# Early routing of prompt rows, dense sample columns and 88-row tiles in a two-layer expert kernel

## The reference, cut to what matters

```python
s = sigmoid(t @ w_router)                        # 16 experts in 4 groups
# group with the largest sum of its two best (s + bias); the two best experts in it
w = s[idx] / s[idx].sum()
h = silu(t @ w_gate[e]) * (t @ w_up[e])          # 1024 -> 512
y = sum over the two experts of w * (h @ w_down[e])   # 512 -> 1024
```

## Time and profile before

| | us |
|---|---|
| three runs | 1125.22 median, 1124.78 to 1127.2 |
| the profiled execution, its own time | 1126.03 |
| its span, first to last instruction | 1124.4 |
| PE busy | 978.1 (87%) |
| DVE busy | 376.1 (33%) |
| ACT busy | 195.2 (17%) |
| POOL busy | 94.5 (8%) |
| bytes moved | 296.26 MB, 263 GB/s in the mean |

### The profile page before, as it was taken

The page is one execution under the profiler, slowest core; times in us unless marked ns, Lnnn a source line. Parts: engine busy times, 40 slices in busy tenths (PEclk is TensorE's granted clock), DMA queues, the critical chain, the costliest instruction groups (busy, mean ns, idle before and its releaser), DMA issues.

```text
span 1124.4 us, 36091 instructions
## 1 busy us (share of the span) xinstructions
PE 978.1 (87%) x15881; PEld 836.7 (74%) x15881; DVE 376.1 (33%) x825; ACT 195.2 (17%) x441; POOL 94.5 (8%) x179
## 2 busy tenths in 40 slices
PE   7979999989998329999999997783399999999975
PEld 6857777754566128999999996562389999999962
DVE  1234443423364612122122122796112122122127
ACT  1233434430052020000000001111200000001010
POOL 0002112141010030000000001200200000000011
PEclk8989999999999559999999999895699999999998
DMA  9513244614311979999999995790599999999935
GB/s 336 189 54 91 89 135 127 206 43 137 92 48 64 412 272 332 361 405 380 403 388 397 381 389 189 269 354 9 194 368 366 407 388 391 393 380 384 396 118 201
DMA packets 80249, 296.26 MB, mean 263 GB/s; under 512 B 10200, under 2 KB 40288, under 8 KB 71871
## 3 DMA queue, kind: packets, MB, share of 16 engines
q1 hardware_dynamic: 52343, 246.53, 58.5%
q10 hardware_dynamic: 19712, 26.75, 7.1%
q0 software_dynamic: 8144, 22.29, 5.7%
HBM read 255.88 MB, written 40.11 MB: 263 GB/s over the span
## 4 chain that ended last, share of the span: by engine, by line
PE 79%; DVE 10%; DMA 4%; issue 3%; POOL 2%; ACT 1%; ACTq 0%; SPq 0%; POOLq 0%; DVEq 0%
PE PS L924 16%; PE PS L945 15%; PE PS L934 15%; PE PS L840 5%; PE PS L598 4%; PE PS L910 3%; PE PS L645 3%; PE PS L661 2%; PE PS L554 2%; PE PS L654 2%; PE PS L576 2%; POOL expert_rows L1106 2%; PE PS L749 1%; PE PS L618 1%; PE PS L635 1%
## 5 line engine op out<-in xcount | busy, mean ns | idle before, releaser
L924 PE MATMUL PS<-arena,ring 128*64 128x96 f32 x4096 | 185.4, 249 | 52.6 <-DVE arena L1759 52.4
L924 PEld LDWEIGHTS PS<-arena,ring 128*64 128x64 f32 x4096 | 175.1, 139 | 59.3 <-issue 59.3
L945 PE MATMUL PS<-arena,ring 128*64 128x96 f32 x4096 | 175.4, 246 | 2.5 <-issue 2.0
L934 PE MATMUL PS<-arena,ring 128*64 128x96 f32 x4096 | 175.0, 246 | 2.8 <-issue 2.8
L945 PEld LDWEIGHTS PS<-arena,ring 128*64 128x64 f32 x4096 | 171.3, 137 | 3.2 <-issue 2.5
L934 PEld LDWEIGHTS PS<-arena,ring 128*64 128x64 f32 x4096 | 171.2, 137 | 3.1 <-issue 3.1
L1759 DVE STREAM_TRANSPOSE arena<-arena 128x768 uint32<-128x768 uint32 x34 | 54.2, 1595 | 166.7 <-ACT arena L1311 138.4
L1784 DVE COPY arena<-PS 128x384 f32<-128x384 f32 x32 | 17.9, 558 | 164.3 <-PE PS L945 164.3
L1313 ACT ACTIVATE arena<-PS 128x384 f32<-128x384 f32 x32 | 15.7, 490 | 265.5 <-PE PS L945 265.5
L840 PE MATMUL PS<-ring,arena 128*128 128x512 f32 x128 | 55.6, 593 | 0.7 <-issue 0.7
L598 PE MATMUL PS<-arena,ring 128*128 128x260 f32 x192 | 46.8, 395 | 2.3 <-POOL ring L1057 2.0
(11 more groups left out here) (276 smaller groups left out, 1030.1 us busy)
## 6 DMA issues: line engine op xcount, KB each, us to landing
ring<-w_gate SPq DMA_DIRECT2D x32, 2048.0 KB, 14.8
ring<-w_up SPq DMA_DIRECT2D x32, 2048.0 KB, 16.1
ring<-w_down SPq DMA_DIRECT2D x32, 2048.0 KB, 17.9
arena<-expert_rows ACTq DMA_DIRECT2D x144, 96.0 KB, 9.0
expert_out<-arena ACTq DMA_DIRECT2D x32, 384.0 KB, 11.8
expert_rows<-ring SPq DMA_DIRECT2D x6, 1920.0 KB, 10.2
ring<-cache_ckv SPq DMA_DIRECT2D x56, 128.0 KB, 2.2
ring<-w_o SPq DMA_DIRECT2D x1, 4096.0 KB, 19.3
```

What stands on the lines that cost most here:

```text
L924: last = nc.tensor.matmul(bank(s, KF, CAP)[at:at + 64, f, :], wg[w][:, k, P * f + at:P * f + at + 64], xeT[s][:, k, :], start=(k == 0), st ...
L934: last = nc.tensor.matmul(out[at:at + 64, :], wu[w][:, k, P * f + at:P * f + at + 64], xeT[s][:, k, :], start=(k == 0), stop=(k == KD - 1))
L945: last = nc.tensor.matmul(bank(4 + m // 4, 4, CAP)[at:at + 64, m % 4, :], wd[w][:, f, P * m + at:P * m + at + 64], h[s][:, f, :], start=(f ...
```

## The change

Three things are changed together.

1. **Early routing.** `route` is split into `choose` (two best experts) and `assign` (slots, indices, tables), each over a range of row blocks. In layer one they run for the four prompt blocks inside `samples()`: `router(0, 3)` moves to batch 1, `choose` behind `sample_pair(1)`, the counting matmuls to PE's batch 2, `assign` behind `sample_pair(2)`. POOL scatters the prompt rows right then (8 of 10 transfers), SP instead of ACT loads the first two tiles, and SP issues the first weights in another order, each as soon as its part of the ring is free. ACT scales the prompt rows before the samples' norm.
2. **Dense sample columns.** The sample rows are routed after the loop has begun. Experts 0 and 1 (tiles 0 and 1, outside of the loop now) compute all 8 sample rows as 8 more columns (WIDE = 104), with an output block of their own (`yT_s`, `ys_s`, 16 rows in `yd`). For the other experts 8 slots are kept free (`reserve`). `choose` and `assign` for the sample block run on DVE during tile 0; their scatter is waited for by ACT in tile 1, before it loads tile 2.
3. **Rows per tile.** ROWS = (96, 88): layer two's tiles stand 88 slots apart, an expert overflows beyond 88 rows, and the gate, up and down matmuls, the silu, the products and the copies there take 88 columns. The load of a tile's input stays at 96 rows; the store is 88 rows. Two more overflow tiles are provided for (NOV = 12).

The diff, cut to its core:

```diff
-NOV = 10
+NOV = 12
+DENSE = 2
+WIDE = CAP + DB
+ROWS = (CAP, 88)
@@ SP, first weights of layer one
-                    load_expert(0, 0, 1, gate_free=(pv_ps, BATCHES + 1))
-                    load_expert(0, 1, 0, gate_free=(mix_ps, NT), down_free=(lg_ps, 1))
+                    sp.wait_ge(pv_ps, 3)
+                    sp.dma_start(wu[1], t["w_up"][0, 0].rearrange("(p k) f -> p k f", p=P)).then_inc(q["wu_ld"][1], 16)
+                    sp.wait_ge(pv_ps, 4)
+                    sp.dma_start(wd[1], t["w_down"][0, 0].rearrange("(k p) d -> p k d", p=P)).then_inc(q["wd_ld"][1], 16)
+                    sp.wait_ge(sc_ps, BATCHES)
+                    sp.dma_start(wd[0], t["w_down"][0, 1].rearrange("(k p) d -> p k d", p=P)).then_inc(q["wd_ld"][0], 16)
+                    sp.wait_ge(pv_ps, 5)
+                    sp.dma_start(wg[1], t["w_gate"][0, 0].rearrange("(p k) f -> p k f", p=P)).then_inc(q["wg_ld"][1], 16)
+                    sp.wait_ge(scat, 128)
+                    load_rows(sp, 0, 0, slice(0, CAP))
+                    load_rows(sp, 0, 1, slice(CAP, 2 * CAP))
+                    sp.wait_ge(mix_ps, NT)
+                    sp.dma_start(wg[0], t["w_gate"][0, 1].rearrange("(p k) f -> p k f", p=P)).then_inc(q["wg_ld"][0], 16)
+                    sp.dma_start(wu[0], t["w_up"][0, 1].rearrange("(p k) f -> p k f", p=P)).then_inc(q["wu_ld"][0], 16)
@@ PE, samples()
-                    if u == BATCHES - 1:
+                    if u == 1:
+                        pe.wait_ge(tp_ev[0], 15)
+                        pe.wait_ge(tp_ev[1], 15)
                         router(0, 3)
+                    elif u == 2:
+                        counts(1, 0, NT - 1)
@@ PE, experts(L)
+                if L == 0:
+                    pe.sem_inc(q["back_ps"], 1)
+                    pe.wait_ge(dense, 2)
+                    tile(0, 0, WIDE)
+                    tile(0, 1, WIDE)
+                    turn_sample_out()
-                with pe.Fori(0, nh) as u:
+                with pe.Fori(1 if L == 0 else 0, nh) as u:
@@ PE, before experts(0)
             mix(0, 4)
+            turn_sample_rows()
             router(0, 4)
-            counts(0)
             experts(0)
@@ DVE, samples()
+                    elif u == 1:
+                        v.memset(r_exp[:, E * (NT - 1):], 1.0).then_inc(lg_zero, 1)
+                        choose(0, 1, 0, NT - 1)
+                    elif u == 2:
+                        assign(0, 1, 0, NT - 1)
@@ PE, tile: every matmul of the three products
-                                last = nc.tensor.matmul(bank(s, KF, CAP)[at:at + 64, f, :], wg[w][:, k, P * f + at:P * f + at + 64],
-                                                        xeT[s][:, k, :], start=(k == 0), stop=(k == KD - 1))
+                                last = nc.tensor.matmul(bank(s, KF, n)[at:at + 64, f, 0:m], wg[w][:, k, P * f + at:P * f + at + 64],
+                                                        x[:, k, :], start=(k == 0), stop=(k == KD - 1))
@@ ACT, behind the four batches
+                act.wait_ge(scat, 128)
+                for i in range(NT - 1):
+                    scale_rows(i)
@@ ACT, tile
+                    if n == WIDE and s:
+                        act.wait_ge(scat, 160)
+                        load_rows(act, L, 0, slice(2 * CAP, 3 * CAP))
+                        scale_rows(NT - 1)
```

More of the change, by code:

```diff
@@ L954, in tile @@
                     down(4, (KF - 1,))
-                    for m in (1, 2, 3, 5, 6, 7):
-                        last = down(m, range(KF))
-                        if m in (3, 7):
+                    for c in (1, 2, 3, 5, 6, 7):
+                        last = down(c, range(KF))
+                        if c in (3, 7):
                             last.then_inc(q["down_ps"][s], 1)
@@ L1035, in _ @@
                 router(1, i)
-            counts(1)
+            counts(3, 0, NT)
             experts(1)
@@ L1348, in samples @@
                         take_latent_out(u - 1)
-                    if u == BATCHES - 2:
+                    if u == 1:
                         take_rows(0, 3)
+                        act.wait_ge(lg_ps, 1)
+                        nc.scalar.activation(r_exp[:, 0:E * (NT - 1)], bank(6, E * (NT - 1)), ACT.Exp, scale=-1.0
+                                             ).then_inc(lg_exp, 1)
                 take_latent_out(BATCHES - 1)
+                act.wait_ge(scat, 128)
+                for i in range(NT - 1):
+                    scale_rows(i)
             deviation(0, 0, 0)
@@ new lines, in by_group, with choose, tiles @@
+            def by_group(a):
+                return a.rearrange("p (a b) -> p a b", b=EPG)
+            def choose(L, n, a, b):
+                T, cols, groups = b - a, slice(E * a, E * b), slice(GROUPS * a, GROUPS * b)
+                over = [P, T, E]
+                def tiles(r):
+                    return r[:, cols].rearrange("p (a b) -> p a b", a=T)
+                dve.wait_ge(lg_exp, n)
+                link(v.tensor_scalar_add(r_exp[:, cols], r_exp[:, cols], 1.0))
+                link(v.reciprocal(r_s[:, cols], r_exp[:, cols]))
+                if n == 1:
+                    dve.wait_ge(router_ld, 32)
+                link(v.tensor_tensor(tiles(r_bias), tiles(r_s), bias_row.unsqueeze(1).to_broadcast(over), ALU.add))
+                b4 = by_group(r_bias[:, cols])
+                sums = r_m6.rearrange("p (a b) -> p a b", b=6)[:, groups, :]
+                cmp = r_big.rearrange("p (a j i) -> p a j i", j=EPG, i=2 * EPG)[:, groups, :, :]
+                wide = [P, T * GROUPS, EPG, EPG]
@@ new lines, in tile @@
+                    if n == WIDE and s == 0:
+                        assign(0, 2, NT - 1, NT)
+                    elif n == WIDE:
+                        next_rows()
+                    dve.wait_ge(q["down_ps"][s], 2 * u + 2)
+                    if n == WIDE:
+                        v.tensor_copy(yT_s[:, 4:8, DB * s:DB * (s + 1)], bank(5, 4, n)[:, :, CAP:])
+                    v.tensor_copy(yT[:, 4:8, 0:ROWS[L]], bank(5, 4, n)[:, :, 0:ROWS[L]]).then_inc(q["yT_set"], 1)
+                tile(0, 0, False, CAP if L else WIDE)
@@ L1820, in _ @@
                     norm(1, 0, step - 4)
-            route(1)
+            choose(1, 3, 0, NT)
+            assign(1, 3, 0, NT)
             dve.wait_ge(mix_ps, 2 * NT)
```

400 lines of the change are left out of this document (225 added, 175 removed).

## The result

The changed kernel takes 1143.2 us in the median (1139.33 to 1144.68), the kernel before beside it on the same chip 1125.07. The ratio is 1.0153, 95% interval 1.0131 to 1.0175: **slower by 1.5%**, where I had forecast 1109.5, 1.4% faster. The profiled execution has a span of 1143.0 us and an own time of 1144.68, the longest of the four.

What follows compares the result with a forecast made beforehand. Layer one's loop waits on the samples' routing chain; layer two is bound by transfers. Early start -18.8, loop one +5.4, between layers +0.3, layer two -2.8 sum to -15.9 us: 1109.5 us forecast, range 1101 to 1119.

Steps and rivals of the forecast that it cites:

- Layer two, -2.8: Layer two's loop: 88 rows a tile save 2.8 us, bounds 0 and 7, because transfers bind rather than PE.
- the store is 32 KB of 7.1 MB smaller (13 x 0.1 us = 1.3): Layer two's output store: fewer bytes per tile save 1.3 us over thirteen tiles, part of the 2.8 us.
- paid in full: Rival, 6%: in layer two transfers have room, so PE's saving of 17.7 us counts whole; 1092 us.
- pace does not follow the columns: Rival, 3%: weight loads set PE's pace, so layer two keeps 17.0 us a tile, -0.3 instead of -2.8; 1112 us.
- overflow: Rival, 4%: an expert in layer two exceeds 88 rows, adding two tiles, 36.8 us; 1146 us.
- turned at about 431, wanted at 434: Layer one, tile 2: its input rows are ready in time; if that cover is gone, a wait up to 4 us.
- The third rival: 15%: early routing gives little, through costlier batches, late tile 2 rows or cold code; together 8 to 12 us less, 1117 to 1121.
- They land by 377. Not on the path.: The eight early prompt scatters before layer one's loop: landed by 377, the two tiles' rows by 385, delaying nothing.
- Low clock, 1.5: Samples' stage after the batches: PE's idle gap brings the lower clock sooner, costing 1.5 us, bounds 0 and 4.
- The batches, 11.9: Samples' batches: routing work in DVE's queue ends the samples' stage 11.9 us later, bounds 10 to 14.
- Cold code, 3.0: Layer one's loop, entered after two unrolled tiles: code is new twice, costing 3.0 us, bounds 0 and 8.
- don't bind here: Layer one's loop: transfers don't set its pace, since they start 20 us earlier as well.

Runs made afterwards that it cites:

- e4: Changed kernel with layer two's 88-row store cut into one transfer of 80 rows and one of 8; 1132.9 us, ratio 1.0063 to the kernel before.
- e11: Kernel before, without early routing, with 88 columns in layer two's matmuls and copies but slots and stores of 96 rows; 1124.7 us, ratio 0.9984.
- e15: e13 with only w_gate of tile 0 and w_down of tile 1 issued behind the prompt scatters' landing; 1116.7 us, ratio 0.9903 to the kernel before.
- e8: e3 with assign's weights and tables moved behind the samples' values and ACT's scalings behind the norm; 1130.3 us, ratio 1.0026 to the kernel before.
- e7: e3 with POOL's two broadcast loads at tile 5 and tile 3's rows issued only when tile 2's are turned; 1124.9 us, ratio 0.9993.
- e5: Changed kernel with latent_q in 64 half-width records in place of 32 full-width ones; 1138.4 us, ratio 1.0093 to the kernel before.
- e9: e3 plus the changes of e5, e7 and e8, and tile 1's output copied before tile 2's rows are turned; 1121.2 us, ratio 0.9959.
- e12: e3 with tile 1's output copied before tile 2's rows are turned and POOL's two broadcast loads at tile 5; 1126.8 us, ratio 0.9978.
- e3: Changed kernel with 88 columns in layer two but slots, capacity and stores at 96 rows; 1134.2 us, ratio 1.0056 to the kernel before.
- e14: e13 with w_gate and w_down of tile 0 and w_down of tile 1 issued only behind the prompt scatters' landing; 1116.9 us, ratio 0.9910.
- e13: e9 with ACT issuing tile 3's rows behind tile 1's output copies, not ahead of them; 1116.7 us, ratio 0.9899 to the kernel before.

## Why the prediction was wrong, step by step

The median is 33.7 us above the forecast. The two largest steps that failed stand first.

- **Layer two, -2.8: measured +8.4.** The failed step is "the store is 32 KB of 7.1 MB smaller (13 x 0.1 us = 1.3)". I priced the store by its bytes; as one transfer of 88 rows it is cut into 11 shares and not 16 (the packet counts above), and every tile took 0.56 us longer than with 80 + 8 rows (e4). The rest was right: with 96-row stores the columns alone give -3.3 in the kernel before (e11), 18.28 us a tile against my 18.4, 37.9 ns a record. One premise of the sum was not: that transfers are served more slowly with a deep queue (see the last section). The rivals "paid in full", "pace does not follow the columns" and "overflow" are all refuted; none of them was this mechanism, and my bounds, 0 to -7, ended on its other side.
- **The rows of tile 2, "turned at about 431, wanted at 434".** Turned at 455.5, and 12.1 us of that are the later start of the loop; wanted at 446.6. In the trace before, sixteen such loads around the loop's start (405 to 445) land in 2.4 us in the median, and I counted with little more. Here they go out beside 2 MB weights with four more row loads and two broadcasts about them, and the broadcasts I had not counted at all. My "up to 4 us" was 9.5 of idle time. The third rival named this cause, too small. The same wait carried loop one past my own sign of being wrong (over 288).
- **"They land by 377. Not on the path."** The scatters landed at 396.4 (e15 shows why), and held first ACT, 1.7 us, and with that gone the rows (e8).
- **latent_q** stood in the change and had no term: 2 to 3.5 us. `mix(0, 3)` behind it ran 2.3 us longer at the lower clock, which had no term either, and whose cause is open.
- **Low clock, 1.5:** 3.3 in the samples' values and projection (0.51 over 370 to 394). Inside its bounds.
- **The batches, 11.9:** 12.0 measured, partly by luck: batch by batch +3.2, +2.4 and +6.4 against my +3.0, +3.5 and +5.3, so two errors of 1 us cancel. My sign "above 401 (the batches cost more)" came true for other reasons. Right were between the loops (0.3 against 0.1), 44.6 ns at 104 columns, 1.7 for the sample output (1.8 in e7), no overflow tile, and tile 0 not waiting for the sample's routing.
- **Cold code, 3.0:** four stalls put down to issue in the first four tiles, 4.65 us in all, against three of 2.53 before: 2.1 more. In bounds; that they are code arriving is my reading, which no run tests.
- **The loop's transfers, "don't bind here":** true of the profiled execution up to its last tile (0.55 us), but not of e5, whose last four tiles took 18.7 to 19.0 us, nor of e9 and e12 to e15.

In sum the early routing with the dense columns does move the first gate record forward, by 11.7 us in the median of seven traces against three without it (402.1 against 413.8; 6.7 in the profiled execution, 18.8 forecast), and loop one loses some 15 to 17 again; e7 gives 9.1 of that back against e3.

## What to carry to other kernels

When a tile's row count changes, read how each of its transfers is cut, not only its bytes: a row count with a poor divisor on one small store can cost more than the columns save. Price small transfers by the queue that they will stand in at their new time; a latency read in a quiet stretch says nothing beside weight loads. And once weights run at their limit, a faster start can be worth nothing in the end, as in e14 and e15, so ask first how much lead the ring has.

## What was not expected of the hardware

- 352 KB a tile stored as one transfer of 88 rows made the loop 8.7 us longer than the same rows stored as 80 and 8, with the DMA share at 1.02 in both; the packets of 4 bytes are 11 a store in the one and 24 in the other.
- Scatters of 128 rows land in 6.7 us with one 2 MB transfer ahead of them (e15) and in 8.8 to 18.0 with three about them (e13); 96 KB row loads in 6.4 us beside weights, in 19.7 with two 512 KB broadcasts and four more loads about them.
- 32 records of 16 columns with 128 columns of weights take 4.1 us at a granted clock of 0.90 (e3, 127 ns each) and up to 5.7 at a lower one; 64 records with 64 columns take 2.0 us (e5, 32 ns each, clock 0.99).
- In e3 the transfers were slow in passing: w_down landed every 19.8 us for two tiles from 914 to 954, and every 17.9 us from 971 to 1079 with 30 us from issue to landing. e11 has the same, 19.6 us twice from 911 to 950; the cause is open. A deep queue was not served more slowly, against what I had read from the earlier trace rows.
